# The last six chunks of a down projection in half units: all row tiles of the first 512 tokens, then of the rest

## The reference, cut to what matters

```python
def _rms_norm(x, g):
    y = xf * lax.rsqrt(jnp.mean(xf * xf, axis=-1, keepdims=True) + EPS)
    return (y * g).astype(x.dtype)
...
for l in range(DEPTH):                       # DEPTH = 2 here
    ...
    h = h + _conv_glu(_rms_norm(h, ffn_norm_g[l]), w_gate_up[l], conv_w[l], conv_b[l], w_down[l])
return _rms_norm(h, final_norm_g)            # (1, 1024, 1024) f32

# in _conv_glu: D_FF = 2816 = 22 chunks of 128
    return (jax.nn.silu(g) * u) @ w_down     # (1024 x 2816) @ (2816 x 1024)
```

## Time and profile before

| | |
|---|---|
| time of the profiled execution | 3114.48 us |
| its span, first to last instruction | 3112.6 us |
| median of the three timed runs | 3114.37 us |
| PE busy | 2986.6 us (96%) |
| DVE, ACT, POOL busy | 2200.9, 1497.8, 705.8 us |
| mean granted TensorE clock | 0.984 |
| last six chunks of the down projection, layer 1 | PE from 3023.76 to 3089.3 us |

### The profile page before, as it was taken

How to read it: one execution, slowest core, us unless ns; L and a number is a source line. 1 busy time by engine, 2 the same in 40 slices (tenths; PEclk the granted TensorE clock), 3 DMA queues, 4 the chain that set the end, 5 groups by cost and what they waited for, 6 DMA issues and landing times.

```text
span 3112.6 us, 40671 instructions
## 1 busy us (share of the span) xinstructions
PE 2986.6 (96%) x15080; PEld 2483.1 (80%) x15080; DVE 2200.9 (71%) x3593; ACT 1497.8 (48%) x2557; POOL 705.8 (23%) x386
## 2 busy tenths in 40 slices
PE   7998999999999999999999989899999999999998
PEld 5787886788887888888777978768888788888877
DVE  6677887442459999988547787763443799999783
ACT  6368866432444333344324797653333533334442
POOL 1122026322131222211221300552212222222021
PEclk9999999999999999999999989999999999999999
DMA  6553750433351222264354467204325322224542
GB/s 217 160 161 96 153 123 20 146 102 102 65 119 62 84 89 89 85 213 145 101 140 122 130 157 152 59 26 149 125 72 115 75 82 82 81 82 142 173 132 75
DMA packets 314051, 350.34 MB, mean 113 GB/s; under 512 B 21872, under 2 KB 244592, under 8 KB 313344
## 3 DMA queue, kind: packets, MB, share of 16 engines
q1 hardware_dynamic: 298912, 314.20, 34.7%
q0 software_dynamic: 6656, 16.78, 2.9%
q10 hardware_dynamic: 8288, 16.78, 1.6%
HBM read 270.04 MB, written 111.21 MB: 122 GB/s over the span
## 4 chain that ended last, share of the span: by engine, by line
PE 76%; DVE 9%; ACT 9%; issue 3%; DMA 2%; SPq 0%; POOL 0%; DVEq 0%; ACTq 0%; POOLq 0%
PE ps L2309 29%; PE ps L2574 8%; PE ps L2575 8%; PE ps L2576 8%; ACT above L1161 4%; PE ps L2344 3%; PE ps L2588 3%; PE ps L2590 3%; PE ps L2589 3%; PE ps L2498 2%; PE ps L2439 2%; PE ps L2376 1%; PE ps L2491 1%; PE ps L2377 1%; PE ps L2548 1%
## 5 line engine op out<-in xcount | busy, mean ns | idle before, releaser
L996 POOL TENSOR_TENSOR w_lo<-raw,w_hi 128x1024 fp32r<-128x1024 f32 (+4 forms) x124 | 267.3, 2162 | 846.2 <-ACT w_hi L1083 844.6
L2309 PE MATMUL ps<-xs_hi,w_hi 128*128 128x512 f32 (+2 forms) x1344 | 419.3, 393 | 11.4 <-POOL w_lo L996 8.5
L2309 PE MATMUL ps<-xs_lo,w_hi 128*128 128x512 f32 (+2 forms) x1344 | 416.6, 391 | 0.0
L2309 PE MATMUL ps<-xs_hi,w_lo 128*128 128x512 f32 (+2 forms) x1344 | 415.8, 391 | 0.0
L2309 PEld LDWEIGHTS ps<-xs_hi,w_hi 128*128 128x128 f32 (+2 forms) x1344 | 250.3, 188 | 70.7 <-issue 12.3
L2309 PEld LDWEIGHTS ps<-xs_lo,w_hi 128*128 128x128 f32 (+2 forms) x1344 | 252.4, 188 | 55.5
L2309 PEld LDWEIGHTS ps<-xs_hi,w_lo 128*128 128x128 f32 (+2 forms) x1344 | 251.9, 187 | 55.3
L1040 POOL TENSOR_SCALAR p_a<-p_a,rca 128x1024 f32<-128x1024 f32 (+7 forms) x96 | 178.4, 1869 | 423.7 <-DVE rca L1938 423.7
L2574 PE MATMUL ps<-xs_hi,w_hi 128*128 128x512 f32 x672 | 262.3, 390 | 3.7 <-DVE xs_lo L2101 3.5
L2575 PE MATMUL ps<-xs_lo,w_hi 128*128 128x512 f32 x672 | 261.7, 389 | 0.0
L2576 PE MATMUL ps<-xs_hi,w_lo 128*128 128x512 f32 x672 | 261.4, 389 | 0.0
(11 more groups left out here) (359 smaller groups left out, 6955.9 us busy)
## 6 DMA issues: line engine op xcount, KB each, us to landing
raw<-in_w_gu SPq DMA_DIRECT2D x48, 512.0 KB, 4.6
act_spill<-cv SPq DMA_DIRECT2D x44, 512.0 KB, 6.0
raw<-in_w_in SPq DMA_DIRECT2D x32, 512.0 KB, 5.8
qk_spill<-t_hi SPq DMA_DIRECT2D x24, 512.0 KB, 2.6
qk_spill<-t_lo SPq DMA_DIRECT2D x24, 512.0 KB, 2.8
k_b<-qk_spill SPq DMA_DIRECT2D x32, 384.0 KB
gate_e<-in_w_gu SPq DMA_DIRECT2D x20, 512.0 KB, 4.1
up_e<-in_w_gu SPq DMA_DIRECT2D x20, 512.0 KB, 5.3
```

The lines of the kernel that those rows point to most:

```text
L996: nc.gpsimd.tensor_tensor(w_lo[s][:, w], raw[s][:, w], w_hi[s][:, w].bitcast(f32), ALU.subtract).then_inc(lo_done, 1)
L2309: ins = M(dst[0:c, a:b], w[s][:, k * c:(k + 1) * c], xt[:, a:b], start=(at == 0 and w is w_hi and part == 0), stop=(at == kc - 1 and w is ...
```

## The change

In both layers the eight units of 36 matmuls become sixteen half units of 18. The first eight take the first 512 tokens of all row tiles, the next eight the other 512. Each half unit loads and splits the same 128x768 weights as the whole one did, so every weight block is loaded and split twice. In layer 0, ACT's `gained` and `square` stay 1024 wide and are done in the second eight. In the last layer all work on the result is done by halves, and the column sums, roots, transposes and scaling of token blocks 0 to 3 are put among the second eight half units: column sums behind half unit 1, block 0 behind 2, 1 behind 3, 2 behind 4, 3 behind 5. Behind half unit 7 come block 4, the other column sums, and blocks 5 to 7.

```diff
-    for g, n in enumerate(FG):
-        u += [("down", (g, m), n, P) for m in range(KC)]
+    for a in range(2):
+        u += [("down", (a, m), FG[0], P) for m in range(KC)]
...
+FINAL = {1: [("ssqc", 3)], 2: [("Y", 0)], 3: [("Y", 1)], 4: [("Y", 2)], 5: [("Y", 3)], 7: [("Y", 4), ("ssqc", 4), ("Y", 5), ("Y", 6), ("Y", 7)]}
+def after_unit(l, a, m):
+    return FINAL.get(m, []) if l == DEPTH - 1 and a == 1 else []
...
@@ scalar (ACT)
+            def square_half(a, k):
+                N, t = NORMS * DEPTH, slice(HALF * a, HALF * a + HALF)
...
+                if k >= 1:
+                    act.wait_ge(acc_done, 7 * N + 7 * a + max(k - 2, 0))
+                A(acc[:, t] if k == 0 else sq[:, k % 2, t], h_t[:, k, t], ACT.Square).then_inc(sq_done, 1)
+            def last_roots(a):
+                job, t = ("ssqc", 3 + a), slice(4 * a, 4 * a + 4)
+                wait_full(act, job)
+                A(rcol_l[:, t], bank(job)[:, t], ACT.Ln, scale=1.0 / D, bias=eps[:, 0:1]).then_inc(drained_of(job), 1)
+                wait_drained(act, job)
+                A(rcol[:, t], rcol_l[:, t], ACT.Exp, scale=-0.5).then_inc(rcol_ready, 1)
+                act.wait_ge(rcol_ready, DEPTH + 1 + a)
...
-                for g, ng in enumerate(FG):
+                for g in range(2):
                     for m in range(KC):
                         if g or m:
                             split_hi(U_AT["down", (g, m)] + 1)
...
+                        if l + 1 < DEPTH:
+                            if g:
+                                wait_drained(act, ("unit", U_AT["down", (g, m)]))
+                                gained(l + 1, G_MIX, m)
+                                square(NORMS * (l + 1), m)
+                            continue
                         wait_drained(act, ("unit", U_AT["down", (g, m)]))
-                        if l + 1 < DEPTH:
-                            gained(l + 1, G_MIX, m)
-                        square(NORMS * (l + 1), m)
+                        square_half(g, m)
+                        if g and m == 2:
+                            last_roots(0)
+                        if g and m in (3, 5):
+                            tokens_out(m - 3)
+            last_roots(1)
+            tokens_out(4)
+            tokens_out(6)
@@ vector (DVE)
+                for g in range(2):
+                    t = slice(HALF * g, HALF * g + HALF)
                     for m in range(KC):
-                        residual(U_AT["down", (g, m)], m)
+                        job = ("unit", U_AT["down", (g, m)])
+                        wait_full(dve, job)
+                        V.tensor_tensor(h_t[:, m, t], h_t[:, m, t], bank(job)[:, t], ALU.add).then_inc(drained_of(job), 1)
                         if l + 1 < DEPTH:
-                            if m:
+                            if g and m:
                                 gained_low(l + 1, G_MIX, 0, m - 1)
...
+                            if g and m >= 2:
+                                add_square(NORMS * (l + 1), m - 1)
+                            continue
+                        wait_drained(dve, job)
+                        V.tensor_scalar(y_fin[:, m, t], h_t[:, m, t], gf[:, m:m + 1], None, ALU.mult).then_inc(y_done, 1)
                         if m >= 2:
-                            add_square(NORMS * (l + 1), m - 1)
+                            add_square_half(g, m - 1)
+                        if g and m in (4, 6):
+                            tokens_out(m - 3)
@@ tensor (PE)
-                for m in range(KC):
-                    project(U_AT["down", (0, m)], chunks=0, ready=(lambda k: after(pe, alo_done, k + 1)) if m == 0 else None)
...
+                for n in range(DOWN, U):
+                    a, m = UNITS[n][1]
+                    project(n, chunks=0, half=a, ready=(lambda k: after(pe, alo_done, k + 1)) if n == DOWN else None)
+                    for kind, i in after_unit(l, a, m):
+                        if kind == "ssqc":
+                            ssq_columns(i, range(4 * (i - 3), 4 * (i - 2)))
+                        else:
+                            pe.wait_ge(y_done, KC * (1 + i // 4))
+                            turn((kind, i), lambda k: y_fin[:, k, i * P:(i + 1) * P], i)
```

More of the change, by code:

```diff
@@ L202, in layer_jobs @@
     j += [("D", p, i) for p in range(NPR) for i in range(2)]
-    j += [("unit", n) for n in range(DOWN, len(UNITS))]
+    for n in range(DOWN, len(UNITS)):
+        j += [("unit", n)] + after_unit(l, *UNITS[n][1])
     return j
@@ L242 @@
 JOBS = [(0, "X", tb) for tb in range(NB)] + [(l, *job) for l in range(DEPTH) for job in layer_jobs(l)]
-JOBS += [(DEPTH - 1, "Y", 0), (DEPTH - 1, "ssqc", 3)] + [(DEPTH - 1, "Y", tb) for tb in range(1, NB)]
 J = {name: n for n, name in enumerate(JOBS)}
@@ L945, in _ @@
                     prev, (grp, k) = (g - 4) // U, UNITS[(g - 4) % U][1]
-                    if prev < DEPTH - 1 and grp == len(FG) - 1:
+                    if prev < DEPTH - 1 and grp == 1:
                         wait_drained(sp, ("unit", (g - 4) % U), prev)
@@ L1092, in square, with tokens_out @@
                 A(acc[:, :] if k == 0 else sq[:, k % 2, :], h_t[:, k, :], ACT.Square).then_inc(sq_done, 1)
+            def square_half(a, k):
+                N, t = NORMS * DEPTH, slice(HALF * a, HALF * a + HALF)
+                if k == 0 and a == 0:
+                    act.wait_ge(acc_done, 7 * N)
+                    wait_full(act, ("ssq", (N - 1) % NORMS), (N - 1) // NORMS)
+                if k >= 1:
[8 more added lines that the diff above has]
+                act.wait_ge(rcol_ready, DEPTH + 1 + a)
+            def tokens_out(tb):
+                job = ("Y", tb)
+                wait_full(act, job)
+                A(tok_out[:, tb, :], bank(job)[:, :], ACT.Copy, scale=rcol[:, tb:tb + 1]).then_inc(drained_of(job), 1)
             def gained(l, at, k):
@@ L1532, in _ @@
                             split_hi(U_AT["down", (g, m)] + 1)
-                        if m == 0 and l + 1 < DEPTH:
+                        if g == m == 0 and l + 1 < DEPTH:
                             act.wait_ge(cs_out, 16)
@@ L1537, in _ @@
                             act.dma_start(cs_raw[:, :, :], cs_spill[:, :, :]).then_inc(cs_in, 16)
-                        wait_drained(act, ("unit", U_AT["down", (g, m)]))
-                        if l + 1 < DEPTH:
-                            gained(l + 1, G_MIX, m)
-                        square(NORMS * (l + 1), m)
[L1543 to L1547, removed]
+                        if l + 1 < DEPTH:
[4 more added lines that the diff above has]
+                            continue
+                        wait_drained(act, ("unit", U_AT["down", (g, m)]))
+                        square_half(g, m)
[6 more added lines that the diff above has]
+            tokens_out(6)
         @block.vector
@@ L2255, in _, with add_square_half, tokens_out @@
                     wait_drained(dve, ("D", NPR - 1, i))
-                for g, ng in enumerate(FG):
+                def add_square_half(a, k):
+                    N, t = NORMS * DEPTH, slice(HALF * a, HALF * a + HALF)
+                    dve.wait_ge(sq_done, KC * N + KC * a + k + 1)
+                    if k > 1:
+                        dve.wait_ge(acc_done, 7 * N + 7 * a + k - 1)
+                    V.tensor_tensor(acc[:, t], acc[:, t], sq[:, k % 2, t], ALU.add).then_inc(acc_done, 1)
+                def tokens_out(tb):
+                    job = ("Y", tb)
+                    dve.wait_ge(rcol_ready, DEPTH + 1 + tb // 4)
+                    wait_full(dve, job)
+                    V.tensor_scalar(tok_out[:, tb, :], bank(job)[:, :], rcol[:, tb:tb + 1], None, ALU.mult).then_inc(drained_of(job), 1)
@@ L2262, in _ @@
                                 gained_low(l + 1, G_MIX, 0, m - 1)
-                        else:
-                            wait_drained(dve, ("unit", U_AT["down", (g, m)]))
-                            V.tensor_scalar(y_fin[:, m, :], h_t[:, m, :], gf[:, m:m + 1], None, ALU.mult).then_inc(y_done, 1)
-                        if m >= 2:
-                            add_square(NORMS * (l + 1), m - 1)
+                            if g and m >= 2:
+                                add_square(NORMS * (l + 1), m - 1)
@@ L2269, in _ @@
                     gained_low(l + 1, G_MIX, 0, KC - 1)
[L2270 to L2276, removed]
+                    add_square(NORMS * (l + 1), KC - 1)
+            tokens_out(5)
+            tokens_out(7)
@@ L2289, in claim, with project @@
                 return ps[j % SETS]
-            def project(n, hi=xs_hi, lo=xs_lo, cols=T, ready=None, chunk_read=None, chunks=None, order=None):
+            def project(n, hi=xs_hi, lo=xs_lo, cols=T, ready=None, chunk_read=None, chunks=None, order=None, half=None):
                 _, _, kc, c = UNITS[n]
@@ L2298, in project @@
                 start_of = {min(ks, key=order.index): i for i, ks in enumerate(parts(n))}
-                halves = [(a, min(a + HALF, cols)) for a in range(0, cols, HALF)]
```

(5 more changed lines are left out.)

11 lines of the change are left out of this document (4 added, 7 removed).

## The result

The changed kernel takes 3126.66 us (median of 6 runs, 3124.3 to 3127.91); the kernel before, timed beside it, 3114.95 us (6 runs, 3113.69 to 3116.43). The ratio is 1.0032, 95% interval 1.0022 to 1.0042: slower, beyond the 0.2% that can be told from no change. The profiled execution took 3127.72 us with a span of 3126.1 us. The forecast was 3122.2 us, with a range of 3117 to 3128.

A forecast was written before the change was run, and what follows sets the result against it. PE, busy 96% of the span, was taken to pace each unit. Layer 0 8.2, last layer's waits 1.8 + 1.8 + 0.5, insertions 4.8, tail -9.3 gave +7.8 us: 3122.2 us, range 3117 to 3128.

The forecast's parts named there:

- The chain of the split in layer 0: Layer 0's second eight and layer 1's first unit: low split done at t + 5.55, after PE's slot; 8.2 us lost.
- The first eight of layer 0: Layer 0's first eight half units: low split done at t + 2.81, before PE's slot at t + 3.88; no wait.
- the 6.3: Weight loads of the half units: longest landing time, 6.3 us; it would cost 0.5 us once.
- the steady state's margin of 5.8 us: Last layer's weight loads: 5.8 us from issue until wanted, against landing in 3.3 us; hidden.
- The last layer's waits: PE waiting for splits in the last layer: 1.8 us in short waits, 1.8 behind the roots, 0.5 at half unit 7.
- The insertions: Transposes and column sums put among the last layer's second eight, on PE's path: 4.8 us, bounds 4.4 and 9.
- The tail: From the last residual add to the end: 14.0 us instead of 23.3, a gain of 9.3.
- The even balance of the last layer: Last layer's waits and inserted work against its shorter tail: -0.4 us by itself.
- Rival A: Splits keep pace, so no wait is added: 4.8 - 9.3 = -4.5 us, 3110.0; chance 0.08.
- Rival B: PE's clock falls at the new waits: +5 us if three of five bring it down, 3127; chance 0.14.
- Rival C: DVE holds off POOL's split; four splits in layer 0 start 1.2 us late: +4.8 us, 3127; chance 0.07.
- Rival D: Blocks 0 to 3 scaled late, their stores queue at the end; tail gains 4.1, not 9.3: 3127.5; chance 0.03.

The follow-up runs named there:

- Experiment 2: Changed kernel with ACT's high split of half unit n+2 ahead of its work on n's result, both layers: 3114.54 us, ratio 0.9993 to before.
- 3: Changed kernel with layer 0 back to eight whole units, last layer still in sixteen half units: 3116.43 us, ratio 1.0001 to before.
- 5: Changed kernel with layer 0's 1 MB cs_raw load issued in the second eight: one run, first eight 32.8 us, second eight 40.4.
- 4: Changed kernel with layer 0 in whole units and the split ahead in the last layer alone: 3112.30 us, ratio 0.9989 to before.
- 6: Two edits of 4: stores held until block 4 is scaled, last-layer stage 89.15 us for 83.96; blocks 0 to 3 behind the last half unit, 3111.08 us.
- the second profile: The changed kernel run again with nothing edited: median 3127.58 us, ratio 1.0037 to before.
- the third profile: The kernel before, run once more with nothing edited for a third profile: 3118.0 us.

## Why the prediction was right

**The chain of the split in layer 0**: right in each link, 5.51 for 5.55, 10.0 for 10.12 per pair, three pairs and the first projection: C is 7.8 above before (predicted 8.2). Experiment 2 shows that it is this chain and nothing else of the sixteen units, 3 that with it the whole loss of the stages is in layer 0.

**The first eight of layer 0**: the step that failed. "Hidden; the 6.3 would cost 0.5 once" took the steady state's margin of 5.8 us for every load. The first load inside the stage goes out when the first low split is done, 1505.0, and is wanted at t = 1509.56: 4.6 us; and it went out beside the 1 MB of cs_raw, which I had not priced, since ACT issues it there in both kernels. In the kernel before this was hidden: the load went out at 1499.75, t was 1508.40, 8.7 us later, and ACT split only at 1511.66. The two loads that went out there between 1499 and 1503 us were no faster:

```profile
DMA to landing us min/median/max: 4.6/5.4/6.2
```

It cost 0.9 to 1.0 us, shown by 5, where 0.5 once was the most that I had allowed.

**The last layer's waits**: 4.4 for 4.1, in short waits of about 0.2 us that cost some 0.45 a pair with the restart, and one of 1.60 behind the roots. **The insertions**: 4.7 for 4.8; the earlier trace rows has 33 transposes in 3.38 us, so eight are 0.82, where the prediction took 0.88. **The tail**: 13.9 for 14.0. The even balance of the last layer was right for the reasons given, which 3, 4 and 6 take apart. That it came out at -0.4 to the tenth is luck: in the second profile, with the granted clock at 0.50 in the tail, it was +0.3.

**Rival A**, the splits keep pace, did not happen, but 2 is the kernel in which it does: layer 0 exact to 0.1 us and the sum of the stages 4.8 below before (predicted 4.5), of which the median shows 1.4. **Rival B**: after waits of 1.61 and 1.57 us in the first profile, 1.62 and 1.60 in the second, and 1.9 at layer 1's start, the clock stayed at 1.00 each time, as in this stretch of the first profile:

```profile
1538.86:1579.25 40.39, 33.79 (x145) 26.40 (x144) 21.95 (x21) 21.89 (x24) 14.87 (x8) 1.00 0.50 159
```

Over the four profiles that hold such waits there are sixteen of 1.47 to 1.87 us, none with a fall behind it. But the length of the idle time doesn't tell what follows, and the earlier trace rows should not be read as if it did. The wait of 1.55 us shown there, behind which the clock stayed at 1.00, stands at the same instruction in every profile, with 1.53 to 1.55 us. In seven of the eleven the granted clock fell to 0.50 within 2 us of it; the kernel before, second profile, is one:

```profile
1658.69 0.50 PE L2376 MATMUL ps<-k_idx,q_idx 128*128 128x512 f32 x1 [1.55 <-ACT relu_b L1246]
...
1660.20:1663.60 3.40, 3.40 (x11) 2.73 (x10) 3.19 (x6) 1.31 (x3) 0.00 (x0) 0.50 0.38 114
```

The other way about, in the third profile PE had been idle for 2.33 us before 1483.41, and the clock stayed at 1.00 for the next 6.6 us, where 2.01 was followed by a fall. So that rival B did not happen is shown for these waits; why not is open. **Rival C** is real, but off the path: DVE's first pass behind a split took 1.90 for 1.28 us, as it began while POOL was splitting, and POOL's low splits never started late by it. **Rival D** did not happen.

**The size of the whole** is less well explained than the parts. The medians differ by 11.7 us in both comparisons, the stages by 8.4. The intervals of the two ratios reach down to 1.0022 and 1.0024, 6.9 and 7.5 us, so 8.4 is within; A and D lie 5 to 11 us apart in single executions, and no trait of the changed kernel is seen in them. But in all six comparisons with more than one run the median lies higher against before than the stages do, by 0.9 (layer 0 whole) to 3.4 us (split ahead in both layers, blocks 0 to 3 at the end), and draws should also fall the other way. Four of the six share one set of times of before, but the three sets agree within 1 us. A and D together average 2959.1 us in the three profiles of before and 2960.6 in the eight of edited kernels, each scattering by some 2.6: too few to tell 1.5 us from none. So the cause of these 3 us is open: draws, or something that the edited programs have in common outside the three stages.

## What to carry to other kernels

A ring of two slots gives each unit's preparation one unit of time. Halving the units without halving what is prepared (here the weights) halves that time: add up the chain from one result to the next slot, with all that its engines do ahead of it in program order, before cutting. An instruction that feeds the bound engine belongs ahead of those that only use its results: moving one line took 13 us off the changed kernel (1 us of it by the load that moved along).

When a tail is bound by its stores, what counts is when the first one starts, and that all engines then stay ahead of the queues. Moving work of the bound engine ahead of its last unit pays only if it takes more off the tail than it puts on that engine's path: here 3.7 us bought 1.0.

## What the runs showed of the hardware that I had not expected

The lock between DVE and POOL works in both directions. In experiment 2 POOL's low split came 0.44 us after DVE had started an instruction with two SBUF inputs, and lasted 2.55 us instead of 1.84; in the changed kernel DVE's `y_fin` (0.49 us elsewhere) came 0.23 us behind a split and lasted 1.85.

```profile
1542.69 1.28 DVE L1617 SCALAR_TENSOR_TENSOR xs_lo<-h_t,packs,xs_hi 128x1024 fp32r<-128x1024 f32 x1
...
1543.13 2.55 POOL L1004 TENSOR_TENSOR w_lo<-raw,w_hi 128x768 fp32r<-128x768 f32 x1 [2.23 <-ACT w_hi L1091]
```

```profile
3091.53 1.85 DVE L2324 TENSOR_SCALAR y_fin<-h_t,gf 128x512 f32<-128x512 f32 x1
```

Both agree with what the Trainium skill (SBUF — State Buffer, "SBUF: two separate sides") says of the pair: whoever starts first has it for the whole instruction. By the rows, POOL's split ended 1.71 us after DVE's instruction, and `y_fin` 0.28 us after POOL's split, each the later of its pair. `y_fin` reads one tensor in SBUF, so it doesn't take two inputs for DVE to be held. Neither was on the path here; in experiment 2, 0.7 us of the 1.1 us that the split ahead had to spare went to it.

The stages outside the change varied by 11 us (A from 1494.2 to 1505.1) from one execution to the next, in good part by where the granted clock was low in the first 60 us: the 200th matmul already starts anywhere from 63.0 to 69.1 us. A change of a few microseconds is better read from stages cut at the same matmul than from the total, as long as the total is compared too: here it kept 1 to 3 us that the stages don't explain.
